# Squares of the first token group's second to fourth x tile one and two slots later, and its turning by TensorE in slots 8 to 15 with two k tiles in each

## The reference, cut to what matters

```python
def rmsnorm(x, g):
    y = xf * lax.rsqrt(jnp.mean(xf * xf, axis=-1, keepdims=True) + EPS)
    return y * g
h = rmsnorm(x, ln_gain[l])
proj = h @ w_in[l]
mem_h = rmsnorm(mem, mem_ln_gain[l])
kv = mem_h @ w_mem_kv[l]
```

## Time and profile before

| what | us |
|---|---|
| median of the three runs | 2632.93 |
| lowest and highest of them | 2632.32 and 2636.37 |
| the profiled execution, its own time | 2637.96 |
| its span, from the first instruction to the last | 2636.1 |
| busy time of TensorE | 2587.3 (98%) |
| of VectorE, ScalarE, GpSimd | 1787.6, 1272.3, 1766.1 |

### The profile page before, as it was taken

One profiled execution on the slowest core, in us unless ns is written; L12 is line 12 of the kernel. 1 busy time (PEld: TensorE's weight loads), 2 busy tenths in 40 slices (PEclk: granted clock), 3 DMA queues, 4 the chain that ended last, 5 costly groups with the idle time before them and its releaser, 6 DMA issues.

```text
span 2636.1 us, 33898 instructions
## 1 busy us (share of the span) xinstructions
PE 2587.3 (98%) x12092; PEld 2136.7 (81%) x12092; DVE 1787.6 (68%) x2217; ACT 1272.3 (48%) x2661; POOL 1766.1 (67%) x1238
## 2 busy tenths in 40 slices
PE   7999999999999999999999999999999999989999
PEld 6878888788887788878888888778888888878887
DVE  4457674576745757457577867878488775878777
ACT  6445454545544455445454454444444454444443
POOL 6577667776677856778545776767476676766666
PEclk9999999999999999999999999999999999999999
DMA  8576767777666776676776443255654444324544
GB/s 255 168 265 213 240 176 246 244 224 238 183 238 239 228 237 192 229 248 213 237 213 210 159 148 99 85 164 176 192 168 152 144 144 129 96 95 144 176 128 136
DMA packets 323853, 492.27 MB, mean 187 GB/s; under 512 B 17943, under 2 KB 134757, under 8 KB 317541
## 3 DMA queue, kind: packets, MB, share of 16 engines
q1 hardware_dynamic: 209076, 299.25, 37.0%
q10 hardware_dynamic: 114608, 190.85, 21.4%
HBM read 367.61 MB, written 97.25 MB: 176 GB/s over the span
## 4 chain that ended last, share of the span: by engine, by line
PE 87%; DVE 6%; POOL 2%; ACT 1%; DMA 1%; issue 1%; SPq 0%; ACTq 0%
PE acc L1777 14%; PE acc L1779 13%; PE acc L1778 13%; PE acc L1849 7%; PE acc L1851 7%; PE acc L1853 7%; PE ps_s L1849 2%; PE ps_s L1853 2%; PE ps_t L1849 2%; PE ps_z L1849 2%; PE ps_t L1851 2%; PE ps_z L1853 2%; PE ps_z L1851 2%; PE ps_t L1853 2%; PE ps_o L1849 2%; PE ps_s L1851 2%
## 5 line engine op out<-in xcount | busy, mean ns | idle before, releaser
L736 POOL TENSOR_TENSOR w_lo<-raw,w_hi 128x512 fp32r<-128x512 f32 x896 | 1255.3, 1412 | 787.5 <-ACT w_hi L859 782.4
L859 ACT ACTIVATE w_hi<-raw 128x512 fp32r<-128x512 f32 x896 | 557.1, 629 | 929.8 <-PE acc L1779 376.3
L1777 PE MATMUL acc<-w_hi,h_hi 128*128 128x512 f32 (+1 forms) x1024 | 377.6, 369 | 12.5 <-POOL w_lo L736 12.5
L1778 PE MATMUL acc<-w_lo,h_hi 128*128 128x512 f32 (+1 forms) x1024 | 373.9, 365 | 0.0
L1779 PE MATMUL acc<-w_hi,h_lo 128*128 128x512 f32 (+1 forms) x1024 | 373.6, 365 | 0.0
L1777 PE MATMUL acc<-h_hi,w_hi 128*128 128x512 f32 x768 | 311.0, 405 | 0.0
L1779 PE MATMUL acc<-h_hi,w_lo 128*128 128x512 f32 x768 | 299.6, 390 | 0.0
L1778 PE MATMUL acc<-h_lo,w_hi 128*128 128x512 f32 x768 | 299.4, 390 | 0.0
L1658 DVE TENSOR_TENSOR a_lo<-s_sum,a_hi 128x512 fp32r<-128x512 f32 x192 | 219.4, 1175 | 36.8 <-ACT a_hi L1145 33.3
L1777 PEld LDWEIGHTS acc<-w_hi,h_hi 128*128 128x128 f32 x1024 | 194.7, 190 | 46.1 <-POOL w_lo L736 14.1
L1779 PEld LDWEIGHTS acc<-w_hi,h_lo 128*128 128x128 f32 x1024 | 194.8, 190 | 30.9
(11 more groups left out here) (277 smaller groups left out, 5432.3 us busy)
## 6 DMA issues: line engine op xcount, KB each, us to landing
raw<-in_w_in SPq DMA_DIRECT2D x256, 512.0 KB, 4.5
raw<-w_sums SPq DMA_DIRECT2D x128, 512.0 KB, 3.7
w_sums<-stage ACTq DMA_DIRECT2D x32, 1024.0 KB, 5.1
probs_t<-blocks_t SPq DMA_DIRECT2D x384, 64.0 KB, 3.0
raw<-in_w_out SPq DMA_DIRECT2D x48, 512.0 KB, 3.7
stage<-in_w_in ACTq DMA_DIRECT2D x32, 512.0 KB, 5.2
h_rows<-early ACTq DMA_DIRECT2D x16, 1024.0 KB, 5.3
half_rows<-ungated ACTq DMA_DIRECT2D x16, 1024.0 KB, 8.5
```

Source lines behind the costliest of these rows:

```text
L736: nc.gpsimd.tensor_tensor(w_lo[:, at, :], raw[:, slot_mod, HALF * half:HALF * half + HALF], w_hi[:, at, :].bitcast(F32), ALU.subtract).the ...
L859: nc.scalar.activation(w_hi[:, 2 * (slot_mod % 2) + half, :], raw[:, slot_mod, HALF * half:HALF * half + HALF], ACT.Copy).then_inc(hi_read ...
L1777: nc.tensor.matmul(dst, st[0], mv[0], start=first, stop=False)
L1778: nc.tensor.matmul(dst, st[0], mv[1], start=False, stop=False)
```

## The change

The squares of the second, third and fourth x tile move from slots 3, 4 and 5 to slots 4, 6 and 7, and with them the inverse roots, which follow one slot on: from slots 4, 5 and 6 to 5, 7 and 8. The first k tile is turned in slot 8, not 7, and each of slots 8 to 15 turns two. The other two edits follow from it: the wait for the vectors stands in the slot that holds k tile 0, and DVE, which used to make `first_low(0)` ahead of `key_means`, now makes none ahead of it; ahead of `key_scale` it has made four, not five.

```diff
-FIRST_TURNS = [[]] * 7 + [[0], [1, 2], [3, 4], [5, 6], [7, 8], [9], [10, 11], [12, 13], [14, 15]]
+FIRST_TURNS = [[]] * 8 + [[2 * n, 2 * n + 1] for n in range(8)]
 K_TURN_MEM = 12
-FIRST_SQUARE_AT = {0: 0, 1: 1, 2: 2, 3: 3, 4: 4, 5: 5}
+FIRST_SQUARE_AT = {0: 0, 1: 1, 2: 2, 4: 3, 6: 4, 7: 5}
@@
-                if s == FIRST_TURNS.index([0]):
+                if 0 in FIRST_TURNS[s]:
                     act.wait_ge(vecs_ready, 2)
@@
-            before_keys = FIRST_TURNS[SB_SLOTS - 1][-1] + 1
+            before_keys = sum(len(turns) for turns in FIRST_TURNS[:SB_SLOTS])
             for k in range(before_keys):
                 first_low(k)
```

## The result

| | before | after |
|---|---|---|
| median (10 runs each) | 2634.82 us | 2641.66 us |
| lowest and highest | 2632.32, 2636.82 | 2639.04, 2643.23 |
| profiled execution, its span | 2637.96, 2636.1 | 2642.28, 2640.4 |
| busy time of TensorE | 2587.3 | 2587.3 |

The changed kernel is slower by 0.25% (ratio 1.0025, 95% interval 1.0015 to 1.0035), or 6.8 us by the medians. The forecast was 6.3 us slower, with 0.65 on "slower by over 0.2%"; its 2639.2 us stood on a median of 2632.93 from three runs, which ten runs put at 2634.82.

A forecast was written before the change was run, and what follows sets the result against it. TensorE bounds the kernel, through its idle time in the first stage. Group 0 begins at 54.5 + 30.18 - 2.85 + 1.8 = 83.6, against 77.32, 6.3 us later; 2632.93 + 6.3 = 2639.2 us, range 2635.3 to 2641.7.

The forecast's parts named there:

- What bounds: TensorE bounds the kernel; only its 14.3 us idle in the first stage is touched, and later work hardly absorbs changes.
- What it removes: Slots 7 and 8, with fewer squares ahead: begin at 39.9 and 44.0, against 41.33 and 47.55; a 3.6 us gain.
- the step about the queue: DMA queue: piece 9 stays behind the bias store, issued some 1.6 us earlier, and lands at 45.4, between 44.1 and 45.7.
- the prediction's own sign: Piece 9's transfer: the prediction is wrong if it lands before 44.
- the queue gives all of it back: Rival on piece 9: store issued 1.6 us earlier, landing as much earlier, at 44.1; +5.0 us, 2637.9; chance 0.14.
- The chain from piece 9 to the first turn: ACT, POOL and DVE from piece 9's landing at 45.4 to the first turn at 54.5, against 47.14 before.
- The step about the ports: POOL and DVE share ports: `low(8)` and `low(10)` meet scalings, taking 3.50 and 3.46 us; alone `low(10)` takes 2.50.
- The idle time and the clock: TensorE idle 7.7 us ahead of the first turn, 46.8 to 54.5; then slot 9 costs 1.8 us more from lower clock.
- The rival in which the low clock lasts on into slot 10: Rival: low clock lasts past slot 9, or piece 9 is held by the store's earlier start; +8.1 us, 2641.0; chance 0.10.
- The pieces costed at nothing: `key_means` ahead of `first_low`, keys' root ahead of `low(11)`: no cost, TensorE hides piece 11, ready at 62.7.
- The earlier slots pay: Rival: last tile scaled in time for a turn right behind slot 8 at 46.8; -3.6 us, 2629.3; chance 0.04.
- A later wait takes it up: Rival: a later TensorE wait on `w_lo`, up to 3.1 us, absorbs part of the loss; +3.2 us, 2636.1; chance 0.05.

The follow-up runs named there:

- store_late: The changed kernel with the bias store issued behind piece 10's load instead of ahead of piece 9's; ratio to before 1.0019.
- last_alone: The changed kernel with the second and third x tile's squares back in slots 3 and 4, only the fourth moved, to slot 7; ratio to before 1.0014.
- second profile: The changed kernel run and profiled once more, with nothing altered; ratio to before 1.0025.
- turns_alone: The changed kernel with the squares of before, in slots 3, 4 and 5, so that only the turns move; ratio to before 0.9993, in a repeat 0.9994.
- spread: The changed kernel with the squares in slots 3, 5 and 6 and both last roots behind `low(8)`; ratio to before 1.0009.
- one_slot_on: The changed kernel with the squares in slots 4, 5 and 6 in place of 4, 6 and 7; ratio to before 1.0017.
- lows_first: turns_alone with the first two `first_low` ahead of `key_means` in DVE's list and POOL's root of the keys one slot later; ratio to before 1.0003.

## Why the prediction was right, point by point

**What bounds.** The first stage, and nothing behind it took the loss up: group 0 began 4.2 us later and the span grew by 4.3. The gap of the medians, 6.8, is larger because the profiled execution of before lies 3.1 us above its median and that of after 0.6 above; 2.0 us of the difference is where slot 0 began.

**What it removes.** Slots 7 and 8 were forecast at 39.9 and 44.0 and came at 39.22 and 43.21. In absolute time that is right to 0.8 us. But slot 7 stood 5.17 us behind slot 6, as before (5.26): it hangs on piece 7's transfer, which was issued 1.3 us earlier (25.67) and took 10.3 us, not 9.7, so the gain that I gave it did not come. Slot 8 gained: 9.2 us behind slot 6 in place of 11.5, though not 7.9 as forecast.

**Piece 9.** Here the step about the queue was off. I took 0.3 us of the earlier issue; the store was issued 2.1 us earlier and piece 9 landed 1.8 us earlier, at 43.9 and not 45.4 (SP's issues in order of time, then each transfer's KB and us from issue to landing, answering):

```profile
31.88 0.66 SPq L671 DMA_DIRECT2D bias_rows<-blocks_t  x1
```

```profile
bias_rows<-blocks_t SPq DMA_DIRECT2D x1, 764.0 KB, 10.6
...
raw<-in_w_mem_kv SPq DMA_DIRECT2D x1, 512.0 KB, 11.3
```

By the prediction's own sign, a landing before 44, this step was wrong, by 0.1 us. Of the 2.1 us, 1.6 are the wait for the bias copy, gone as forecast. SP came to piece 7 some 1.3 us earlier, as this whole execution did, and issuing pieces 7 and 8 took 0.8 us longer. Over the thirteen profiles with the store ahead of piece 9, it took 11.0 to 12.4 us from issue to landing, for issues from 31.7 to 34.7. The twelve besides that of before tell the change's part from that of the late start. In the six with no square ahead of the bias copy the store was issued at 31.2 and piece 9 landed at 43.6, by the means; in the six with one, at 32.2 and 44.4. So the landing goes nearly with the issue, and the change makes it some 0.8 us earlier. That was the condition of the rival "the queue gives all of it back". The condition nearly held. Its outcome, 5.0 us slower, lies below both gaps of the medians (6.8 and 7.2) but inside the interval of the ratio, which is 4.0 to 9.2 us, so the times alone do not refute it. The experiment store_late showed that the first turn stays where it is even with the store out of the way. What the Trainium skill's page "DMA: Bandwidth & Descriptors", section "Queues, rings and completion order", says of the order in a ring is not spoken against by this, since what stood ahead in the queue had been issued earlier as well; no run shows the packets' order.

**The chain from piece 9 to the first turn** was forecast at 9.1 us (45.4 to 54.5) and took 9.07 (43.88 to 52.95), link by link 0.71, 2.53, 0.51, 3.44, 0.54 and 1.34. The step about the ports held in it: `low(8)` and `low(10)` met a scaling and took 3.52 and 3.48 us, against 2.48 without one in last_alone. The Trainium skill, page "SBUF — State Buffer", section "Who interferes with whom", has the pair of ports locked for a whole instruction, and the trace agrees.

**The idle time and the clock.** Forecast 7.7 us and 1.8 us. Measured 6.73, and by the time from the first turn to group 0 (28.57 us, against 27.33 = 30.18 - 2.85 with no fall) 1.2 for the clock. The rival in which the low clock lasts on into slot 10 did not come. The second profile went half the way to it: the clock was low for nearly all of slot 9 and cost 2.7 us. It is no other cause but another execution of the same one.

**The pieces costed at nothing.** `key_means` ahead of `first_low(0)` was hidden, by the very wait that was the loss: `first_low(0)` began at 55.66, and the turn that needs its bank at 58.07. Where an experiment took the wait away, that cover went too, and up to 1.96 us came to light. My sentence on what happens "if that cover were gone" named POOL and `low(11)` alone; it should have named this bank.

**The other rivals.** "The earlier slots pay" fell: the wait of 6.73 us stands where the gain should be. "A later wait takes it up" fell. That the sum came out at the measured size, 6.3 against 6.8, has some luck in it. Group 0 was forecast at 83.6 and came at 81.52: 1.5 us of that is the early piece 9, 0.6 the cheaper fall of the clock. Against these 2.1 us stand the 2.0 us by which before's profile had started late, and which the sum took for a part of the kernel. There is luck in the absolute time as well: 2641.66 lies 0.04 us inside the upper end of the range (2641.7) and outside the 2638.2 to 2640.2 of the forecast itself, because the median of before had been taken 1.9 us too low.

## What to carry to other kernels

When a step is moved later in lists written by hand, count what each of its followers now stands behind on the other engines: here a root of half a microsecond got two weight pieces ahead of it, and TensorE waited 6.7 us for it. Slots made earlier gain nothing while something else that they all need arrives late, so look for the latest arrival first. And a cost that is hidden by a wait comes back when the wait is mended: the forecast for the mended kernel has to ask for it anew.

## What the runs showed that I had not expected

- The first stage of one and the same kernel moves by some 2 us from one execution to the next. One source is the start: the first weights landed 2.0 us later in the profile of before. Another is where the clock falls: in slots 0 and 7 in the profile of before (the second fall hidden by the wait for the last scaling), in slot 6 in turns_alone and store_late, in slot 7 in spread, last_alone and the second profile of after, in no slot ahead of the long wait in its first. Two single profiles do not settle a difference of that size.
- The length of the wait just ahead does not tell whether the clock falls. In spread it fell behind a wait of 1.96 us, while in one_slot_on the work behind a wait of 3.44 us ran at 1.00, and so did slot 7 of the first profile of after, behind 2.15 us.
- A DVE instruction on 8 columns (the keys' mean, L1360) took 0.17 us after the change, with POOL idle, and 1.12 to 1.14 us in turns_alone and lows_first, where a low part ran beside it, whose two instructions take 1.25 us each (2.50 the pair). That fits a wait for the whole of the other's instruction.
- TensorE's wait ahead of the first turn does not show one to one in the end: spread removed 6.7 us of it and came out 4.4 us faster than the change, by the medians' distances to before.
